# Gated DeltaNet decode step: two tokens per 32-row group, outer products on four row tiles, block inverse from NT directly

## The chip, the cores and the metric

The kernel runs on one core of a Trainium2 chip. Its metric is the device time of one launch in microseconds (us), the median of repeated runs.

## What is computed

One inference step of a two-layer hybrid decoder trunk in float32, for 256 new prompt tokens and 8 decode tokens (one new token for each of 8 sequences), so that every activation has 264 columns. Layer A is a gated DeltaNet mixer (32 value heads, 16 key heads, head size 128) and a SwiGLU block; layer B is sliding-window attention and another SwiGLU block. The change touches only the DeltaNet mixer. For the prompt it works in chunks, and needs the inverse of a unit triangular matrix for each head and chunk:

```python
a_mat = jnp.where(strict, jnp.einsum('bhnid,bhnjd->bhnij', kb, k) * decay, 0.0)
t_mat = lax.linalg.triangular_solve(a_mat + eye, eye, left_side=True, lower=True)
u = t_mat @ (v * beta[..., None]);  w = t_mat @ (kb * jnp.exp(gc)[..., None])
```

For the 8 decode tokens it carries a 128x128 state S for each token and head:

```python
S = S * jnp.exp(g_t)[..., None, None]
kv_mem = jnp.einsum('bhde,bhd->bhe', S, k_t)
S = S + jnp.einsum('bhd,bhe->bhde', k_t, (v_t - kv_mem) * b_t[..., None])
o = jnp.einsum('bhde,bhd->bhe', S, q_t)
```

## The kernel before

**Weights.** All weights pass through SBUF in 858 pieces of 128x1024 floats. ScalarE rounds a piece to `w_hi` (`split_hi`, line 470), VectorE computes the rest `w_lo` (`split_lo`, line 477), and TensorE multiplies each of the eight 128x128 tiles of a piece three times with 264 columns: `w_hi` by the high and the low part of the activations (lines 498 and 499, in turn), then, for all eight, `w_lo` by the high part (line 503). `w_hi` and `w_lo` have two buffers each, so `split_hi` of piece j+1 waits until TensorE is through with piece j-1.

**Turns.** The mixer runs in 16 groups G of two heads. In one turn of 12 pieces j = 0 to 11 TensorE projects the inputs of group g = G+1 while all engines do the DeltaNet work of group G in steps n = 0 to 23, two to a piece. On TensorE step 2j stands ahead of piece j and step 2j+1 in its middle, after 12 of its products. The last turn (G = 15) has no next group, and its pieces belong to the output projection. All engines take their instructions in the written order. ScalarE does at piece j: steps 4 or 16 where j is 2 or 8, then `split_hi` of piece j+1, then (j = 4, 8) the copies of the projection just ended (`unit_copy`), then steps 2j and 2j+1. VectorE does step 2j, then `split_lo` of piece j+1, then step 2j+1, with the convolution of group g (`conv`) and the decay and norm work (`early`) between; at j = 11 `split_lo` stands first.

**The inverse** (steps 2 to 14) starts from `NT`, the strictly upper matrices of four head and chunk pairs, each 128x128. Blocks of 16 are inverted by series (steps 4 to 7), and then blocks of 32, 64 and 128 are put together from two halves and the block of N between them (steps 8 to 14). Before the change `NT` is transposed on TensorE in step 7 (line 1975) into `Nm`, which ScalarE copies out (line 1709). `UF` is the finished inverse and lies in the same memory as `NT`. ScalarE writes its two 64x64 diagonal blocks for each matrix (line 1715), after which VectorE writes a 32x32 piece beside each (line 2372), and step 13 on TensorE (line 2008) waits for both through `inv_act` and `inv_dve`.

**The decode tokens** (steps 15 to 23): `kv_pad` holds k and v of the eight tokens, repeated three times at 32-column distance, and step 15 transposes it (line 2028). Step 17 multiplies the states by k and q of the tokens, eight products on four 32-column tiles (line 2051). VectorE copies the rows out to `kq_rows` (line 2419), and a product by the constant `gather` in step 18 (line 2062) puts them in place. `dec_d` is the error of the delta rule (lines 2397, 2399), `dec_sel` (line 2401) selects key and query rows, and the product of both (line 2076, step 19) is the output of the decode tokens. `kmask`, which GpSimd writes (line 1459), holds the keys of one token in each 128-column slice, as high part and rest in 96 rows, `dec_dr` holds the errors in like rows, and `outer` (line 1922) multiplies them, two tokens a call with 96 rows of contraction: calls 0 and 1 in step 21, call 2 in step 22, call 3 in step 23. VectorE adds the results to the states (`s_dec`, line 2437). `early` (lines 2107 and 2108), ahead of piece 11, sums the squares of the next keys in bank B[0]; step 23 sums the squares of the outputs (line 2096) and waits, among others, for ScalarE's logarithm of the former (`rn_ln`, line 1675).

## Time and profile before

| | |
|---|---|
| median of 3 runs | 2878.22 us (2877.65 to 2879.23) |
| span of the profiled execution | 2873.6 us |
| TensorE products busy | 2854.6 us, 99% |
| VectorE busy | 1795.8 us, 62% |
| ScalarE busy | 1417.1 us, 49% |
| GpSimd busy | 150.7 us, 5% |
| HBM traffic | 183 GB/s over the span |
| the 16 turns of the mixer | from about 71 to 900 us of the span |

The profiled execution gives its span, from its first to its last instruction, and no time of its own; the 4.6 us between the span and the median of the runs lie outside the instructions. PE is TensorE's products, PEld its weight loads, DVE VectorE, ACT ScalarE, POOL GpSimd. Recorded durations of products overlap their neighbours, so the time that a product takes of the engine is read from the start of the one to the start of the next.

### The profile page before, as it was taken

The page shows a single profiled execution, that of the slowest core. Times are in us where ns is not written, and L with a number is a line of the kernel's source. Part 1 is how long each engine was busy: PE and PEld are TensorE (multiplying, and loading weights), DVE is VectorE, ACT ScalarE, POOL GpSimd, SP SyncE. Part 2 cuts the span into 40 slices and gives each one's busy share as a digit, 9 for nine tenths or more (in the row PEclk, how much of TensorE's full clock was granted, in tenths as well). Part 3 has the DMA queues.
Part 4 walks back from the last instruction along what each step waited for, and adds up shares of the span by engine and source line. Part 5 has one row for each costly group of instructions (what it writes and reads, how often), then busy time and mean ns, then how long its engine had stood idle before and what let it go on. Part 6 is the DMA issues. An engine that isn't in the chain of part 4 may idle for free.

```text
span 2873.6 us, 68820 instructions
## 1 busy us (share of the span) xinstructions
PE 2854.6 (99%) x25511; PEld 2781.0 (97%) x25511; DVE 1795.8 (62%) x2900; ACT 1417.1 (49%) x2141; POOL 150.7 (5%) x285
## 2 busy tenths in 40 slices
PE   8999999999999999999999999999999999999999
PEld 7999999999999999999999999999999999999999
DVE  7888788888886455555555444587555555554444
ACT  6666566565664444444444343566444444444343
POOL 1112112111110000000000000000000000000000
PEclk9999999999999999999999999999999999999999
DMA  7666656666556555555555555744555555555554
GB/s 226 189 178 188 191 166 194 181 177 188 160 182 198 187 188 178 181 180 178 182 179 180 183 180 181 221 151 130 171 182 179 179 182 178 180 182 179 182 180 152
DMA packets 521091, 518.97 MB, mean 181 GB/s; under 512 B 32128, under 2 KB 444201, under 8 KB 520665
## 3 DMA queue, kind: packets, MB, share of 16 engines
q1 hardware_dynamic: 519150, 510.34, 57.6%
q0 software_dynamic: 1152, 5.58, 0.6%
q8 instruction: 147, 2.41, 0.4%
q10 hardware_dynamic: 594, 0.25, 0.0%
q14 instruction: 48, 0.39, 0.0%
HBM read 492.12 MB, written 32.82 MB: 183 GB/s over the span
## 4 chain that ended last, share of the span: by engine, by line
PE 67%; issue 1%; ACT 0%; DMA 0%; DVE 0%; DVEq 0%; ACTq 0%; POOLq 0%
PE bank L498 11%; PE bank L503 11%; PE bank L499 11%; PE upper L503 11%; PE upper L498 11%; PE upper L499 11%; PE upper L1027 0%; PE upper L1052 0%; DMA x_res<-x_spill 0%; PE upper L1038 0%; PE upper L1089 0%; PE upper L1028 0%; PE upper L1055 0%; ACT scores L812 0%; PE upper L1042 0%
## 5 line engine op out<-in xcount | busy, mean ns | idle before, releaser
L477 DVE TENSOR_TENSOR w_lo<-w_raw,w_hi 128x1024 fp32r<-128x1024 f32 x858 | 1051.2, 1225 | 919.9 <-ACT w_hi L470 917.0
L470 ACT ACTIVATE w_hi<-w_raw 128x1024 fp32r<-128x1024 f32 x858 | 910.1, 1061 | 1241.6 <-PE bank L503 709.1
L498 PE MATMUL bank<-h_hi,w_hi 128*128 128x264 f32 x3168 | 829.6, 295 | 0.4 <-DVE h_lo L585 0.3
L499 PE MATMUL bank<-h_lo,w_hi 128*128 128x264 f32 x3168 | 794.8, 284 | 0.0
L498 PEld LDWEIGHTS bank<-h_hi,w_hi 128*128 128x128 f32 x3168 | 597.3, 189 | 21.3 <-issue 8.8
L499 PEld LDWEIGHTS bank<-h_lo,w_hi 128*128 128x128 f32 x3168 | 598.2, 189 | 1.3
L503 PE MATMUL bank<-h_hi,w_lo 128*128 128x264 f32 x3168 | 449.8, 284 | 0.0
L503 PEld LDWEIGHTS bank<-h_hi,w_lo 128*128 128x128 f32 x3168 | 412.1, 188 | 0.0
L498 PE MATMUL upper<-h_hi,w_hi 128*128 128x264 f32 x1456 | 361.7, 285 | 0.0
L499 PE MATMUL upper<-h_lo,w_hi 128*128 128x264 f32 x1456 | 361.4, 284 | 0.0
L498 PEld LDWEIGHTS upper<-h_hi,w_hi 128*128 128x128 f32 x1456 | 274.3, 188 | 0.0
L499 PEld LDWEIGHTS upper<-h_lo,w_hi 128*128 128x128 f32 x1456 | 273.9, 188 | 0.0
L503 PE MATMUL upper<-h_hi,w_lo 128*128 128x264 f32 x1456 | 206.6, 284 | 0.0
L503 PEld LDWEIGHTS upper<-h_hi,w_lo 128*128 128x128 f32 x1456 | 189.3, 188 | 0.0
L498 PE MATMUL upper<-a_hi,w_hi 128*128 128x264 f32 x688 | 170.9, 284 | 0.0
L498 PE MATMUL bank<-a_hi,w_hi 128*128 128x264 f32 x688 | 170.9, 284 | 0.0
L499 PE MATMUL bank<-a_lo,w_hi 128*128 128x264 f32 x688 | 170.7, 284 | 0.0
L499 PE MATMUL upper<-a_lo,w_hi 128*128 128x264 f32 x688 | 170.7, 284 | 0.0
L498 PEld LDWEIGHTS upper<-a_hi,w_hi 128*128 128x128 f32 x688 | 129.7, 189 | 0.0
L498 PEld LDWEIGHTS bank<-a_hi,w_hi 128*128 128x128 f32 x688 | 129.7, 189 | 0.0
L499 PEld LDWEIGHTS bank<-a_lo,w_hi 128*128 128x128 f32 x688 | 129.5, 188 | 0.0
L499 PEld LDWEIGHTS upper<-a_lo,w_hi 128*128 128x128 f32 x688 | 129.5, 188 | 0.0
(447 smaller groups left out, 3655.5 us busy)
## 6 DMA issues: line engine op xcount, KB each, us to landing
w_raw<-in_w_gate_up_dram SPq DMA_DIRECT2D x704, 256.0 KB, 2.9
w_raw<-in_w_in_a_dram SPq DMA_DIRECT2D x388, 256.0 KB, 3.2
w_raw<-in_w_down_dram SPq DMA_DIRECT2D x352, 256.0 KB, 2.9
w_raw<-in_w_out_a_dram SPq DMA_DIRECT2D x128, 256.0 KB, 3.1
s_dec<-in_state_delta_dram SPq DMA_DIRECT2D x32, 512.0 KB, 6.1
out_dram<-s_dec SPq DMA_DIRECT2D x32, 512.0 KB, 4.9
w_raw<-in_w_q_b_dram SPq DMA_DIRECT2D x64, 256.0 KB, 3.1
w_raw<-in_w_o_b_dram SPq DMA_DIRECT2D x64, 256.0 KB, 2.9
```

The lines of the kernel that those rows point to most:

```text
L470: nc.scalar.activation(w_hi[:, s % SPL, :], w_raw[:, s, :], ACT.Copy).then_inc(hi_ready, 1)
L477: ops.tensor_tensor(w_lo[:, s % SPL, :], w_raw[:, s, :], w_hi[:, s % SPL, :].bitcast(F32), ALU.subtract).then_inc(lo_ready, 1)
L498: nc.tensor.matmul(bank[bk][:, 0:T], high(t), xh, start=first, stop=False)
L499: nc.tensor.matmul(bank[bk][:, 0:T], high(t), xl, start=False, stop=False)
L503: m = nc.tensor.matmul(bank[bk][:, 0:T], low(t), xh, start=False, stop=last)
```

## The change

The inverse no longer uses the transpose of `NT`: the transposes of step 7, `Nm` and its copy go, and steps 8 to 14 multiply the other factor, transposed by VectorE (`Tm`), by `NT` itself. ScalarE copies one half of `Um` into `Us`, and its copy of the diagonal blocks into `UF` moves from step 11 to step 12, since step 11 on TensorE now reads the part of `NT` that it overwrites. The transposes of the 32x32 pieces move from step 13 of VectorE to step 12.

In the decode part, each 32-row group holds two tokens with four rows each (key three times, query once), so that the states' products come out in the rows in which they are used. `gather`, `kq_rows` and their product go, and `dec_sel` and `dec_d` move from step 18 to step 17 of VectorE, ahead of `vn`. `kmask` is written by ScalarE (step 17) and VectorE (step 18) in place of GpSimd. The eight outer products have 32 rows of contraction each, on four row tiles, each tile with a bank of its own, all in step 21; `early` waits for the first four updates of the states.

```diff
-            def decode_keys(G):
-                pool.wait_ge(dec_dve, 11 * G + 2)
-                pool.tensor_tensor(kmask[:, :, :], bc(dec_kd.bitcast(F32), 1, NB),
-                                   sel8[0:96, :].unsqueeze(2).broadcast_to([96, NB, P]),
-                                   ALU.mult).then_inc(kmask_ready, 1)
...
                 elif n == 7:
...
                     nc.scalar.activation(twos(Um), pair23, ACT.Copy).then_inc(inv_act, 1)
-                    act.wait_ge(inv_pe, 13 * G + 7)
-                    nc.scalar.activation(Nm[:, :, :], B[0][:, :], ACT.Copy).then_inc(inv_act, 1)
-                elif n == 11:
-
-                    act.wait_ge(inv_dve, 15 * G + 10)
+                    for b in range(2):
+                        at, to = slice(HP * b, HP * (b + 1)), slice(HP * (1 - b), HP * (2 - b))
+                        m = nc.scalar.activation(Us[to, :, :], pair23[at, 1, :].rearrange("p (m n) -> p m n", m=2), ACT.Copy)
+                    m.then_inc(inv_act, 1)
+                elif n == 12:
+
+                    act.wait_ge(inv_pe, 12 * G + 9)
                     for b in range(2):
                         at = slice(HP * b, HP * (b + 1))
                         m = nc.scalar.activation(UF[at, :, at], Um[at, :, :], ACT.Copy)
                     m.then_inc(inv_act, 1)
-                elif n == 12:
-                    act.wait_ge(inv_pe, 13 * G + 11)
-                    nc.scalar.activation(Tm[HP:P, 2:4, :], Tm[0:HP, 2:4, :], ACT.Copy).then_inc(inv_act, 1)
...
                 elif n == 13:
+                    act.wait_ge(inv_dve, 15 * G + 13)
+                    nc.scalar.activation(Um[0:HP, 0:2, :], UF[HP:P, 0:2, HP:P], ACT.Copy).then_inc(inv_act, 1)
                     after(act, on_added, G)
                     nc.scalar.activation(q_sq[:, :], qk[:, 0, :], ACT.Square, scale=float(P * EPS ** 0.5)).then_inc(q_sq_ready, 1)
...
+                elif n == 17:
+
+                    act.wait_ge(dec_dve, 9 * G + 1)
+                    for r in range(2):
+                        m = nc.scalar.activation(kmask[:, r, :], dec_k, ACT.Copy, scale=k_first[r])
+                    m.then_inc(dec_act, 1)
                 elif n == 19:
-                    act.wait_ge(dec_dve, 11 * G + 7)
-                    nc.scalar.activation(dec_dr[:, :, :], dec_d[0:96, :, :], ACT.Copy).then_inc(dec_act, 1)
+                    act.wait_ge(dec_dve, 9 * G + 7)
+                    nc.scalar.activation(dec_dr[:, :, :], dec_d, ACT.Copy, scale=d_first).then_inc(dec_act, 1)
...
-                    for m_ in range(4):
-                        m = nc.tensor.transpose(B[0][:, m_ * P:(m_ + 1) * P], NT[:, m_, :], ident)
-                    m.then_inc(inv_pe, 1)
                 elif n == 8:
 
+                    inv(inv_dve, 8)
                     inv(inv_act, 6)
-                    each4(pair23, full(Nm), half(Um)).then_inc(inv_pe, 1)
+                    each4(pair23, full(NT), half(Tm)).then_inc(inv_pe, 1)
                 elif n == 10:
                     inv(inv_dve, 9)
-                    each4(pair01, half(Tm), half(Xm)).then_inc(inv_pe, 1)
+                    each4(pair01, half(Xm), lambda m_, b: (Um[block(b), m_, :] if m_ < 2 else Us[block(b), m_ - 2, :])
+                          ).then_inc(inv_pe, 1)
...
                 elif n == 11:
 
-                    inv(inv_dve, 10)
+                    inv(inv_dve, 11)
                     for m_ in range(4):
                         for b in range(2):
                             lo, up = quarter(b, 1), quarter(b, 0)
-                            m = nc.tensor.matmul(B[0][up, m_ * QP:(m_ + 1) * QP], Nm[lo, m_, up],
-                                                 Um[lo, m_, QP:2 * QP], start=True, stop=True)
+                            m = nc.tensor.matmul(B[0][lo, m_ * QP:(m_ + 1) * QP], NT[up, m_, lo],
+                                                 Tm[up, m_, 0:QP], start=True, stop=True)
...
                 elif n == 13:
 
                     inv(inv_act, 7)
-                    inv(inv_dve, 13)
+                    inv(inv_dve, 14)
                     for i in range(2):
                         for b in range(2):
                             m_ = 2 * b + i
-                            m = nc.tensor.matmul(B[3][block(b), i * HP:(i + 1) * HP], Nm[block(1), m_, block(0)],
-                                                 UF[block(1), m_, block(1)], start=True, stop=True)
+                            m = nc.tensor.matmul(B[3][block(b), i * HP:(i + 1) * HP], NT[block(0), m_, block(1)],
+                                                 Tm[block(0), m_, :], start=True, stop=True)
...
                     pe.wait_ge(dec_padded, 5 * G + 5)
-                    for i in range(3):
-                        nc.tensor.transpose(B[0][0:96, i * P:(i + 1) * P], kv_pad[:, i, :], ident)
-                    nc.tensor.matmul(B[0][0:96, 3 * P:3 * P + NB], kv_pad[:, 0, :], qk[:, 0, NP:T], start=True,
+                    for i, m_ in enumerate((1, 2, 0)):
+                        nc.tensor.transpose(B[0][:, i * P:(i + 1) * P], kv_pad[:, m_, :], ident)
+                    nc.tensor.matmul(B[0][:, 3 * P:3 * P + NB], kv_pad[:, 0, :], qk[:, 0, NP:T], start=True,
                                      stop=True).then_inc(dec_pe, 1)
                 elif n == 16:
...
-                    pe.wait_ge(dec_dve, 11 * G + 5)
-                    nc.tensor.matmul(B[1][:, 0:2 * P], gather, kq_rows[:, :, :], start=True, stop=True).then_inc(dec_pe, 1)
...
                 elif n == 21:
-                    pe.wait_ge(kmask_ready, G + 1)
-                    pe.wait_ge(dec_dve, 11 * G + 11)
+                    pe.wait_ge(dec_dve, 9 * G + 9)
                     pe.wait_ge(seq_act, 2 * G + 2)
-                    outer(0).then_inc(outer_pe, 1)
+                    pe.wait_ge(dec_act, 3 * G + 3)
                     pe.wait_ge(seq_dve, 7 * G + 7)
-                    outer(1).then_inc(outer_pe, 1)
-                elif n == 22:
-                    pe.wait_ge(outer_dve, 16 * G + 4)
-                    outer(2).then_inc(outer_pe, 1)
+                    for r in range(2):
+                        for c in range(4):
+                            at = slice(32 * c, 32 * c + 32)
+                            m = nc.tensor.matmul(B[c][:, r * 2 * P:(r + 1) * 2 * P], kmask[at, r, :], dec_dr[at, :, :],
+                                                 start=True, stop=True, tile_position=(32 * c, 0))
+                            if r:
+                                m.then_inc(outer_pe, 1)
                 elif n == 23:
                     pe.wait_ge(outer_dve, 16 * G + 8)
-                    outer(3).then_inc(outer_pe, 1)
                     pe.wait_ge(on_sq, G + 1)
                     pe.wait_ge(rn_ln, min(G + 1, GROUPS - 1) + 1)
...
                 if G is not None:
-                    pe.wait_ge(dec_act, 2 * G + 2)
-                    pe.wait_ge(seq_dve, 7 * G + 5)
+                    pe.wait_ge(outer_dve, 16 * G + 4)
                 nc.tensor.matmul(B[0][:, 0:T], ones_r[:, :], k_hl[:, 0, :], start=True, stop=False)
...
                     elif n == 7:
                         dve.wait_ge(inv_act, 9 * G + 5)
-                        nc.vector.transpose(Tm[:, 0:2, :], Um[:, 0:2, :])
-                        for b in range(2):
-                            at, to = slice(HP * b, HP * (b + 1)), slice(HP * (1 - b), HP * (2 - b))
-                            m = nc.vector.transpose(Tm[to, 2:4, :], Um[at, 2:4, :])
-                        m.then_inc(inv_dve, 1)
+                        turned(Tm, Um)
                     elif n == 8:
...
                     elif n == 11:
+                        got(9)
+                        nc.vector.tensor_copy(Xm[:, :, 0:QP], m4(B[0][:, 0:P])).then_inc(inv_dve, 1)
+                    elif n == 12:
                         got(10)
-                        nc.vector.tensor_copy(Xm[0:96, :, 0:QP], m4(B[0][0:96, 0:P])).then_inc(inv_dve, 1)
-                    elif n == 12:
-                        got(11)
                         dve.wait_ge(inv_act, 9 * G + 7)
                         for b in range(2):
                             at = HP * b
                             m = ts(UF[at:at + QP, :, at + QP:at + HP], m4(B[1][at:at + QP, 0:P]), -1.0, None, ALU.mult)
                         m.then_inc(inv_dve, 1)
+                        own(13)
+                        nc.vector.transpose(Tm[QP:HP, :, 0:QP], UF[0:QP, :, QP:HP]).then_inc(inv_dve, 1)
                     elif n == 13:
-                        own(13)
-                        dve.wait_ge(inv_act, 9 * G + 8)
-                        for b in range(2):
-                            at = HP * b + QP
-                            m = nc.vector.transpose(Tm[at:at + QP, 2 * b:2 * b + 2, 0:QP],
-                                                    UF[0:QP, 2 * b:2 * b + 2, QP:HP])
-                        m.then_inc(inv_dve, 1)
-                        got(12)
+                        got(11)
                         nc.vector.tensor_copy(Xm[:, 0:2, :], B[3][:, 0:P].rearrange("p (m n) -> p m n", m=2)
                                               ).then_inc(inv_dve, 1)
...
                     if n == 18:
-                        dve.wait_ge(dec_pe, 4 * G + 3)
-                        dve.wait_ge(dec_dve, 11 * G + 4)
-                        for h in range(2):
-                            stt(dec_d[0:96, h, :], B[1][0:96, h * P:(h + 1) * P], sc_eb[0:96, h, 2:3], dec_d[0:96, h, :],
-                                ALU.mult, ALU.add).then_inc(dec_dve, 1)
-                        nc.vector.tensor_copy(dec_d[96:P, :, :], h2(B[1][96:P, 0:2 * P])).then_inc(dec_dve, 1)
-                        for h in range(2):
-                            stt(dec_sel[:, h, :], ident[:, 96:96 + NB], sc_eb[:, h, 0:1], dec_qk[:, :], ALU.mult,
-                                ALU.add).then_inc(dec_dve, 1)
+                        dve.wait_ge(dec_act, 3 * G + 1)
+                        for r in range(2):
+                            m = stt(kmask[:, r, :], dec_k, k_rest[r], kmask[:, r, :].bitcast(F32),
+                                    ALU.mult, ALU.add)
+                        m.then_inc(dec_dve, 1)
                 elif n == 16:
 
-                    dve.wait_ge(dec_pe, 4 * G + 1)
-                    nc.vector.tensor_copy(dec_kd, B[0][0:96, 0:P]).then_inc(dec_dve, 1)
-                    dve.wait_ge(dec_dve, 11 * G + 1)
-                    tt(dec_kd[64:96], B[0][64:96, 0:P], dec_kd[64:96].bitcast(F32), ALU.subtract).then_inc(dec_dve, 1)
-                    tt(dec_d[0:96, :, :], h2(B[0][0:96, P:3 * P]), sc_eb[0:96, :, 1].unsqueeze(2).broadcast_to([96, 2, P]),
+                    dve.wait_ge(dec_pe, 3 * G + 1)
+                    nc.vector.tensor_copy(dec_k, B[0][:, 2 * P:3 * P]).then_inc(dec_dve, 1)
+                    tt(dec_d, h2(B[0][:, 0:2 * P]), sc_eb[:, :, 1].unsqueeze(2).broadcast_to([P, 2, P]),
                        ALU.mult).then_inc(dec_dve, 1)
-                    tt(dec_qk[0:96, :], B[0][0:96, 3 * P:3 * P + NB], ident[0:96, 0:NB], ALU.mult).then_inc(dec_dve, 1)
+                    tt(dec_qk[:, :], B[0][:, 3 * P:3 * P + NB], key_sel, ALU.mult).then_inc(dec_dve, 1)
                 elif n == 17:
                     dve.wait_ge(seq_pe, 7 * G + 4)
                     for h in range(2):
                         stt(rhs[:, h, :], B[0][:, h * P:(h + 1) * P], sc_n[:, h:h + 1], vtok[:, h, 1, :],
                             ALU.mult, ALU.add).then_inc(seq_dve, 1)
 
-                    dve.wait_ge(dec_pe, 4 * G + 2)
-                    nc.vector.tensor_copy(kq_rows[:, :, :], h2(B[1][:, 0:2 * P])).then_inc(dec_dve, 1)
+                    dve.wait_ge(dec_dve, 9 * G + 3)
+                    for h in range(2):
+                        stt(dec_sel[:, h, :], query_sel, sc_eb[:, h, 0:1], dec_qk[:, :], ALU.mult, ALU.add
+                            ).then_inc(dec_dve, 1)
+                    dve.wait_ge(dec_pe, 3 * G + 2)
+                    for h in range(2):
+                        stt(dec_d[:, h, :], B[1][:, h * P:(h + 1) * P], sc_eb[:, h, 2:3], dec_d[:, h, :],
+                            ALU.mult, ALU.add).then_inc(dec_dve, 1)
                 elif n == 19:
-                    dve.wait_ge(dec_act, 2 * G + 1)
-                    mid = dec_dr[32:64]
-                    tt(mid, dec_d[32:64, :, :], mid.bitcast(F32), ALU.subtract).then_inc(dec_dve, 1)
+                    dve.wait_ge(dec_act, 3 * G + 2)
+                    stt(dec_dr[:, :, :], dec_d, d_rest, dec_dr[:, :, :].bitcast(F32), ALU.mult, ALU.add
+                        ).then_inc(dec_dve, 1)
...
-                    for i in ((0, 1), (2,), (3,))[n - 21]:
-                        dve.wait_ge(outer_pe, 4 * G + (i + 1))
-                        for bb in range(2):
+                    for c in ((0, 1), (2,), (3,))[n - 21]:
+                        dve.wait_ge(outer_pe, 4 * G + (c + 1))
+                        for r in range(2):
                             for h in range(2):
-                                s = s_dec[:, h, 2 * i + bb, :]
-                                at = (2 * bb + h) * P
-                                stt(s, s, sc_eg[:, h, 2 * i + bb:2 * i + bb + 1], B[2 + i % 2][:, at:at + P],
+                                b, at = 4 * r + c, (2 * r + h) * P
+                                stt(s_dec[:, h, b, :], s_dec[:, h, b, :], sc_eg[:, h, b:b + 1], B[c][:, at:at + P],
                                     ALU.mult, ALU.add).then_inc(outer_dve, 1)
```

## Rows read from the trace of the kernel before

**Rows 1.** the page: busy time and share of the span, instructions.

```profile
PE 2854.6 (99%) x25511; PEld 2781.0 (97%) x25511; DVE 1795.8 (62%) x2900; ACT 1417.1 (49%) x2141; POOL 150.7 (5%) x285
```

**Rows 2.** busy time by stretch: us, PE, PEld, DVE, ACT, POOL, clock, DMA, GB/s.

```profile
105.00:889.00 784.00, 783.14 (x8250) 730.01 (x8249) 645.10 (x1397) 480.56 (x896) 131.46 (x238) 1.00 0.63 180
```

**Rows 3.** instructions of line 1998: duration, first and last start.

```profile
L1998 PE MATMUL upper<-Xm,Tm x256: 191/191/212, 93.7 to 871.5; 32*32 32x32 f32 x128
```

**Rows 4.** TensorE in order of time, one turn: start, duration, line, operation.

```profile
497.79 0.46 PE L1907 MATMUL upper<-Um,Pb 64*64 64x64 f32 x16
...
498.18 0.66 PE L1975 MATMUL upper<-masks,NT 128*128 128x128 f32 x4
...
498.59 0.36 PE L498 MATMUL bank<-h_hi,w_hi 128*128 128x264 f32 x1
...
500.22 0.46 PE L1907 MATMUL upper<-Um,Nm 64*64 64x64 f32 x16
...
507.79 0.44 PE L1998 MATMUL upper<-Xm,Tm 32*32 32x32 f32 x16
...
509.82 0.45 PE L2008 MATMUL upper<-NT,Nm 64*64 64x64 f32 x8
```

**Rows 5.** ScalarE in order of time, same turn.

```profile
503.81 1.06 ACT L470 ACTIVATE w_hi<-w_raw 128x1024 fp32r<-128x1024 f32 x1 [0.81 <-PE bank L503]
...
504.78 0.83 ACT L1715 ACTIVATE NT<-Um 64x256 f32<-64x256 f32 x2
...
507.96 1.06 ACT L470 ACTIVATE w_hi<-w_raw 128x1024 fp32r<-128x1024 f32 x1 [2.35 <-PE bank L503]
```

**Rows 6.** VectorE in order of time, same turn, the inverse.

```profile
498.73 0.31 DVE L2351 STREAM_TRANSPOSE Tm<-Um 128x128 f32<-128x128 f32 x1 [0.81 <-ACT Um L1707]
...
508.37 0.58 DVE L2372 TENSOR_SCALAR NT<-upper 32x128 f32<-32x128 f32 x2 [0.62 <-PE upper L1998]
```

**Rows 7.** TensorE in order of time, steps 17 to 19.

```profile
519.11 1.07 PE L2051 MATMUL upper<-s_dec,kq_diag 128*32 128x256 f32 x16
...
521.67 0.66 PE L2058 MATMUL upper<-vn,NT 128*128 128x128 f32 x4
...
522.17 0.60 PE L2062 MATMUL upper<-kq_rows,masks 128*128 128x256 f32 x2
...
522.73 0.28 PE L499 MATMUL bank<-h_lo,w_hi 128*128 128x264 f32 x1
...
524.06 0.38 PE L2068 MATMUL upper<-qdec,S 128*128 128x128 f32 x2
```

**Rows 8.** VectorE in order of time, steps 17 and 18.

```profile
521.48 0.42 DVE L2419 COPY kq_rows<-upper 128x256 f32<-128x256 f32 x1
...
521.81 0.87 DVE L2259 SCALAR_TENSOR_TENSOR cacc<-craw,convw,cacc 128x256 f32<-128x256 f32 x2
...
522.60 0.42 DVE L2390 TENSOR_TENSOR vn<-upper,sc_b 128x256 f32<-128x256 f32 x1
...
523.40 0.60 DVE L2397 SCALAR_TENSOR_TENSOR Pb<-upper,sc_eb,Pb 96x128 f32<-96x128 f32 x2
...
524.49 0.61 DVE L2401 SCALAR_TENSOR_TENSOR dec_sel<-masks,sc_eb,dec_qk 128x8 f32<-128x8 f32 x2
```

**Rows 9.** TensorE in order of time, steps 21 to 23.

```profile
528.74 0.64 PE L1922 MATMUL upper<-dec_dr,kmask 96*128 96x256 f32 x4
...
529.21 0.28 PE L498 MATMUL bank<-h_hi,w_hi 128*128 128x264 f32 x1
...
530.67 0.29 PE L2107 MATMUL upper<-k_hl,ones_r 128*128 128x264 f32 x1
...
532.99 1.06 PE L2096 MATMUL upper<-norm_sq,masks 128*128 128x264 f32 x4
```

**Rows 10.** VectorE and ScalarE in order of time, steps 20 to 22.

```profile
529.78 2.15 DVE L2437 SCALAR_TENSOR_TENSOR s_dec<-s_dec,sc_eg,upper 128x128 f32<-128x128 f32 x8
...
532.36 0.46 ACT L1675 ACTIVATE k_sq<-upper,bias_c 128x264 f32<-128x264 f32 x1
```

120 lines of the change are left out of this document (64 added, 56 removed).

## The prediction

> **What bounds the kernel now.** I read the page's first part, then the busy time by stretch, then one instruction's starts over all turns, and then one turn of each engine in order of time. TensorE is busy 2854.6 of 2873.6 us, and the other engines at most 62% [rows 1]. The stretch that holds the turns but the first and the last shows the same more sharply: TensorE is idle for less than 1 us of 784, at a granted clock of 1.00, and VectorE is busy 645 us, 82% [rows 2]. So in the turns the time is TensorE's queue of work, and an instruction taken from it is worth the step from its start to the next start, as long as nobody makes TensorE wait afterwards. The turns are alike: the block of line 1998, once a turn, starts first at 93.7 and last at 871.5, which is 15 periods of 51.8 us [rows 3]. I therefore work out one turn, in the times of the turn around 490 to 541 us, and multiply. Only the mixer's 16 turns are touched; the other two thirds of the span stay as they are. Start-up has smaller constants to load and one more small table instruction, neither of which I price: TensorE runs on weight pieces there.
>
> With VectorE at 82% and each step waiting for the one before, the second question is which of the many hand-overs has slack. This decides the case, since the change shortens TensorE's work by about 1.3 us a turn and also moves instructions on ScalarE and VectorE.
>
> **Part 1, the transposes of NT.** They take TensorE from 498.18 to 498.59, 0.41 us [rows 4]; they go. What is late next? Step 8 started at 500.22 and would start at 499.81. It needs VectorE's transpose of `Um`, which began at 498.73 and in its new, full width takes one instruction of some 0.45 us (the row has 0.31 for half the width), so it is ready at 499.2 [rows 4, 6]. ScalarE's two half copies into `Us` stand where one wide copy of `Nm` stood. Cover is 0.6 us; I take the whole 0.41 us as gained. The exits from tiled work into full products cost the same after the transposes as after the tiles, so the bounds are narrow: 0.35 to 0.45.
>
> **Part 2, the move of the copies into UF.** This is where I expect the loss. Before, ScalarE copied the diagonal blocks in step 11, at 504.78, in time in which it was idle anyway: its next instruction, `split_hi` of piece 7, started at 507.96, just behind the start of step 12 on TensorE at 507.79, for which it had waited 2.35 us [rows 4, 5]. In the new order the copies stand in step 12, and step 12 stands behind that `split_hi` in ScalarE's queue. They can't start before it is done. From the rows: `split_hi` at 507.96, the copies 0.97 us after it (504.78 less 503.81, the same pair of instructions), so at 508.93; they last 0.83, to 509.76 [rows 5]. VectorE's two scalings of the 32x32 pieces, which began at 508.37, now wait for them and last 0.58: 509.78 to 510.36. Behind them comes the transpose of these pieces, now in one instruction of 32x128, for which I take the 0.31 of the transpose with as many elements a row and 0.03 for the wait on its own predecessor: 510.70 [rows 6]. Step 13 on TensorE waits for it (the count of `inv_dve` is now 14). With 0.06 for the semaphore it starts at 510.76; it started at 509.82 [rows 4]. The loss is 0.94 us in each turn, at a place where TensorE has nothing else in its queue. Both step 12 and `split_hi` count from the same product's end, so that a turn that arrives earlier doesn't shorten it. Bounds: 0.83, if the copies and scalings overlap as neighbours sometimes do, and 1.1, if the restart of a stopped TensorE costs a weight load. Behind VectorE's wait stand `split_lo` of piece 7, half of the convolution and two of `early`; `split_lo` would end near 512, and the piece needs it after 515, so this is covered.
>
> **Part 3, the gather product and the new order on VectorE.** From the start of the product of line 2062 to that of the second weight product behind it are 0.56 us, and a weight product takes 0.12, so it costs 0.44; the block ahead of it, line 2058, took 0.50 to its next start where its like takes 0.45, since the product had waited for `kq_rows` [rows 7]. Together TensorE would be at step 19 by 0.49 us earlier: 523.57 in place of 524.06. But step 19 needs `vn`, and VectorE now does more ahead of it. Gone is the copy of `kq_rows`, 0.33 from start to start (521.48 to 521.81). In its place stand the two of `dec_sel`, 0.54, and the two of `dec_d`, 0.60, from step 18 [rows 8]. So `vn`, which began at 522.60 and took 0.42, is ready at 523.83 and TensorE goes on at 523.9. Of 0.49 us 0.16 is left. Bounds: 0 (were the small instructions slower for the 128 rows in place of 96) and 0.25 (were neighbours to overlap fully).
>
> **Part 4, the outer products.** Before: two calls in step 21, 0.47 us from 528.74 to 529.21, which is 0.12 for each product of 256 columns, and two more calls of some 0.24 to 0.3 in piece 11; about 1.0 us altogether [rows 9]. The price of eight products on row tiles of 32 isn't in the trace; the nearest is line 2051 with column tiles: eight products of plain float32 with 256 columns in 1.07 us [rows 7]. One such untiled product is 0.44 us (line 2062 above), so eight would be 3.5; the tiles work four at a time, and about 0.2 us is lost besides. For the new products, each 0.12 us, I take two rounds, 0.24, and 0.33 for this loss and the two changes of tiling: 0.57 us, 0.10 more than what stood in this place. From above the bound is eight in a row and the same loss, 1.3 us; from below 0.24.
>
> The Trainium skill, TensorEngine Tiling (Array Packing), Theoretical Speedup and Key Properties, gives up to four times the rate for a contraction of 32, and says that a change of tiling mode drains the engine. By the first alone the block would be 0.24 us; by the second too it comes near my 0.57, and the rows of line 2051 agree with both.
>
> But again this stretch isn't TensorE's. ScalarE goes without a gap from `split_hi` at the start of piece 10 through two table-bound functions to the logarithm at 532.36 to 532.82, and step 23 waits for it; it started at 532.99 [rows 9, 10]. VectorE updates the states from 529.78, eight in 2.15 us, so that the fourth ends near 530.9, and `early`, which came at 530.67, now has to wait for it, because bank B[0] takes one of the results. With the 0.16 us of part 3 all of this comes earlier by 0.16: fourth update 530.75 and `early` 530.83; two products 0.24 and twelve of 0.12 bring TensorE to step 23 at 532.5; the logarithm is there at 532.66 and step 23 starts at 532.72. This is 0.27 us earlier than before. So parts 3 and 4 together give 0.27 us a turn and not the 1.0 that TensorE is spared. Bounds: 0 to 0.45. Even products in a row (1.3 us) would only move this to 0.1. Behind this, VectorE is busy without a gap up to step 5 of the next turn and has about the same 0.1 to 0.2 us of slack there, so that no more than this can be passed on.
>
> **What costs nothing:** GpSimd's `kmask` (1.9 us) goes from an engine that idles. ScalarE's two `kmask` copies in step 17 stand before a wait of 1.5 us for piece 8. VectorE in steps 16 to 19 has some 0.3 us less. The state stores wait for all 16 updates as before.
>
> **The sum.** A turn: -0.41 + 0.94 - 0.27 = +0.26 us; fifteen turns +3.9. In the last turn there is no next group and so no convolution in VectorE's way; there I count the gather product in full and 0.4 us for the outer products: -0.41 + 0.94 - 0.49 - 0.4 = -0.36. Together +3.5 us: a span of 2877.1, and, with the 4.6 us outside it as before, 2881.7 us. By bounds a turn lies between -0.07 (0.83 less 0.45 less 0.45) and +0.75 (1.1 less 0.35), which is 2876 to 2889 us. About 0.2% (5.8 us) is what a measurement can tell from no change.
>
> **Rivals.** *The order of ScalarE's queue doesn't bite.* If step 13 isn't held, be it that `split_hi` of piece 7 can start earlier than I read it or that the scalings don't wait long, the turn gets -0.41 - 0.27, in all about -11.5 us: 2866.7. For it: the gain is plain work off a full engine. Against it: the 2.35 us wait in ScalarE's row. Half of the hold would give 2874. *VectorE's chain is the bound and pays nothing back.* If `dec_sel` and `dec_d` ahead of `vn` take 0.2 us more than the rows say, step 19 starts no earlier than before, and if each of the new waits (steps 13, 19, `early`, 23) costs a restart of about 0.1 us, a turn is +0.53 to +0.8, in all 2886 to 2890, slower than before. It decides from the point where `vn` is ready after 524.06 in the turn shown. *The tiles don't run side by side.* That would be 2884, inside my own case.
>
> **Chances.** My case 0.60 (2876 to 2884), the first rival 0.15 with its half form, the second 0.2, a loss elsewhere that I don't see 0.05. Faster by over 0.2% 0.14, within 0.2% 0.60, slower 0.26. Range 2872 to 2889, which leaves out the full form of the first rival and the end of the second.
>
> **What would show it.** In the new trace: no line with `Nm`; TensorE idle for about 0.9 us once a turn, ahead of the first product of step 13, released by VectorE's transpose; ScalarE's copies into `UF` right behind a `split_hi`; small waits of 0.2 to 0.3 us ahead of step 19 (for `vn`) and of `early` (for `s_dec`); the eight outer products within 0.6 us; a period of 52.0 us where it was 51.8. I am wrong if there is no idle time ahead of step 13, or if `vn` comes before TensorE does.

## Result and the profile after

The changed kernel takes 2886.14 us (2884.69 to 2887.95, nine runs); the kernel before takes 2877.65 us (2876.05 to 2879.51, nine runs beside them). The ratio is 1.003, with a 95% interval of 1.0021 to 1.004: the change makes the kernel slower by 8.5 us. It lies in the range of 2872 to 2889, but 2 us above the case that I held likeliest (2876 to 2884) and past the border of 0.2%, and so in the outcome to which I gave 0.26.

The page of the changed kernel, busy time, to be read beside [rows 1]:

```profile
span 2886.1 us, 68598 instructions
...
PE 2845.7 (99%) x25415; PEld 2763.0 (96%) x25415; DVE 1777.9 (62%) x2837; ACT 1425.7 (49%) x2189; POOL 136.2 (5%) x268
```

TensorE does 8.9 us less work and the span is longer. The busy time by stretch says where the rest went; it is the stretch of [rows 2] with the same columns:

```profile
105.00:889.00 784.00, 766.27 (x8106) 706.34 (x8105) 624.11 (x1325) 488.64 (x940) 118.65 (x223) 1.00 0.62 180
```

In the turns TensorE was idle for 0.9 us of 784 before and is idle for 17.7 us now, at the same granted clock of 1.00. The list of what TensorE waited for (us in total, times, the longest; three of its lines) names the place:

```profile
PE upper L2011 <- ACT Um L1725: 15.5, 16, 1.0
...
PE upper L510 <- DVE w_lo L484: 2.4, 1, 2.4
PE upper L2109 <- DVE s_dec L2432: 2.4, 14, 0.2
```

Line 2011 is step 13, sixteen times, once a turn. One turn of TensorE in order of time (start, duration, line, operation, idle time before); step 12 is line 2001, step 19 line 2070, the outer products line 2089, `early` lines 2109 and 2110, step 23 line 2099. A row that the view cut at the edge of its stretch counts only the instructions in it, as the last three `w_lo` products do here (535.28):

```profile
511.97 0.44 PE L2001 MATMUL upper<-Um,Xm 32*32 32x32 f32 x16
...
515.03 0.45 PE L2011 MATMUL upper<-Tm,NT 64*64 64x64 f32 x8 [0.96 <-ACT Um L1725]
...
528.82 0.41 PE L2070 MATMUL upper<-qdec,S 128*128 128x128 f32 x2
...
533.42 0.28 PE L506 MATMUL bank<-h_lo,w_hi 128*128 128x264 f32 x1
533.63 0.51 PE L2089 MATMUL upper<-dec_dr,kmask 32*128 32x256 f32 x8
534.07 0.39 PE L505 MATMUL bank<-h_hi,w_hi 128*128 128x264 f32 x1
534.29 0.29 PE L506 MATMUL bank<-h_lo,w_hi 128*128 128x264 f32 x1
...
535.28 0.52 PE L510 MATMUL bank<-h_hi,w_lo 128*128 128x264 f32 x3
535.97 0.36 PE L2109 MATMUL upper<-k_hl,ones_r 128*128 128x264 f32 x1 [0.17 <-DVE s_dec L2432]
536.17 0.28 PE L2110 MATMUL upper<-k_hl,ones_r 128*128 128x264 f32 x1
...
537.87 0.68 PE L2099 MATMUL upper<-norm_sq,masks 128*128 128x264 f32 x2
```

ScalarE and VectorE in the same turn, around the copies into `UF`, which answer to [rows 5] and [rows 6]:

```profile
512.14 1.06 ACT L477 ACTIVATE w_hi<-w_raw 128x1024 fp32r<-128x1024 f32 x1 [3.09 <-PE bank L510]
513.11 0.83 ACT L1721 ACTIVATE NT<-Um 64x256 f32<-64x256 f32 x2
514.58 0.31 ACT L1725 ACTIVATE Um<-NT 64x128 f32<-64x128 f32 x1 [0.65 <-DVE NT L2373]
...
513.97 0.58 DVE L2373 TENSOR_SCALAR NT<-upper 32x128 f32<-32x128 f32 x2 [2.03 <-ACT NT L1721]
514.58 0.30 DVE L2376 STREAM_TRANSPOSE Tm<-NT 32x128 f32<-32x128 f32 x1
```

This is the chain that was forecast, link by link. `split_hi` of piece 7 starts at 512.14, 0.17 us behind step 12; the copies follow at 513.11; VectorE's scalings, which waited 0.62 us for TensorE before, now wait 2.03 us for these copies; the transpose ends at 514.88 and step 13 starts at 515.03. From step 12 to step 13 it is 3.06 us where it was 2.03 [rows 4]. The wait is listed under ScalarE's line 1725, but in the kernel step 13 waits for VectorE's transpose of line 2376 and not for that copy; both start at 514.58 and end 0.01 us apart, and the list names the later one.

Where do 8.5 us come from? The 16 turns, from the first step 1 to the last step 12, take 806.1 us where they took 800.7: +5.4. The end of the span behind the last step 12 takes 2007.8 where it took 2002.1: +5.7. The start is 1.4 us longer, but it differs by up to 2.8 us between the profiled executions of these kernels. The two spans are 12.5 us apart, 4 us more than the medians: the profiled execution of the kernel before was shorter than the median of its kernel, and that of the changed kernel, with 2887.95 us, the longest of its nine. So the turns are shown at their full size (they differ by 0.2 us at most between two profiles of a kernel), and of the start and the end, 7.1 us in these two profiles, the medians hold only some 3.

### The profile page after: what moved, and what is told of

The parts are those of the page before. It is cut to its first block, busy times and chain, and to the rows that moved or that the text cites. A ratio compares the mean times of both kernels' runs of the same rounds, so it can differ in the third digit from the quotient of the medians.

```text
span 2886.1 us, 68598 instructions
## 1 busy us (share of the span) xinstructions
PE 2845.7 (99%) x25415; PEld 2763.0 (96%) x25415; DVE 1777.9 (62%) x2837; ACT 1425.7 (49%) x2189; POOL 136.2 (5%) x268
## 4 chain that ended last, share of the span: by engine, by line
PE 67%; ACT 1%; DMA 0%; DVE 0%; issue 0%; SPq 0%; DVEq 0%; ACTq 0%; POOLq 0%
PE bank L505 11%; PE bank L510 11%; PE bank L506 11%; PE upper L505 11%; PE upper L510 10%; PE upper L506 10%; PE upper L1034 0%; DMA x_res<-x_spill 0%; PE upper L1059 0%; PE upper L1045 0%; DMA out_dram<-S 0%; PE upper L1096 0%; DVE s_dec L2432 0%; PE upper L1172 0%; PE upper L1035 0%
```

## Experiments

Each is compared with the kernel before, run on the same chip in the same batch (its median lies between 2876.9 and 2877.7 us in the four batches); ratios have a 95% interval. "Turns" is the time from the start of the first step 1 to the start of the last product of the last step 12 in the profiled execution, "end" the span behind it. The last five kernels are made from "copies first".

| kernel | us | ratio | turns | end |
|---|---|---|---|---|
| before | 2877.65 | 1 | 800.7, 800.9 | 2002.1, 2002.7 |
| after | 2886.14 | 1.003 [1.0021, 1.004] | 806.1, 806.2 | 2007.8, 2007.3 |
| inverse only | 2888.17 | 1.0039 [1.0025, 1.0052] | 810.6 | 2004.3 |
| decode only | 2872.78 | 0.9987 [0.9978, 0.9996] | 796.8 | 2002.6 |
| before, copies late | 2888.91 | 1.0042 [1.0028, 1.0055] | 812.0 | 2003.3 |
| after, copies first | 2869.6 | 0.9973 [0.9963, 0.9984] | 790.8 | 2006.4 |
| + tiles in pairs | 2868.95 | 0.9969 [0.9957, 0.9982] | 790.4 | 2006.1 |
| + outer twice | 2869.42 | 0.9972 [0.9962, 0.9983] | 790.4 | 2004.8 |
| + `early` later | 2868.18 | 0.9968 [0.9956, 0.998] | 789.1 | 2005.4 |
| + `qdec` later | 2869.17 | 0.9973 [0.9963, 0.9984] | 790.8 | 2006.4 |
| + both later | 2862.41 | 0.9948 [0.9934, 0.9961] | 783.9 | 2005.6 |

### The cause: which edit holds step 13

**Copies first.** The changed kernel, with ScalarE's step 12 called ahead of `split_hi` of piece 7, as its steps 4 and 16 are in their pieces.

```diff
-                    if j in (2, 8) and G is not None:
+                    if j in (2, 6, 8) and G is not None:
                         step(G, 2 * j)
...
-                        if G is not None and n not in (4, 16):
+                        if G is not None and n not in (4, 12, 16):
                             step(G, n)
```

> The changed kernel, but ScalarE does its copies into UF (step 12) ahead of the split_hi of the same piece, in time in which it idles, instead of behind it. Theory A (the place of these copies in ScalarE's queue is what makes the changed kernel slow): step 13 on TensorE follows step 12 by 2.03 us as in the kernel before and not by 3.06, a turn lasts 51.1 to 51.2 us where the changed kernel has 52.16, and the time is 2886.1 less 16 times 1.03, 2869.6 us; if VectorE's chain swallows a part, up to 2873. Theory B (the decode part with its new order on VectorE and its waits is what costs): the time stays over 2880 us. Theory C (the end of the mixer costs several us by itself, where in the changed kernel's trace TensorE waits 2.4 us once near 922 us): that wait is still there, and the time is some 4 us above what 15 turns explain.

Measured: 2869.6 us, 16.5 us less than the changed kernel, or 1.03 us for each of the 16 turns. The line of step 13 is gone from the list of waits. ScalarE and VectorE of this kernel, in order of time:

```profile
500.75 0.84 ACT L1721 ACTIVATE NT<-Um 64x256 f32<-64x256 f32 x2 [1.39 <-PE upper L1993]
502.44 1.06 ACT L477 ACTIVATE w_hi<-w_raw 128x1024 fp32r<-128x1024 f32 x1 [0.85 <-PE bank L510]
...
502.86 0.58 DVE L2373 TENSOR_SCALAR NT<-upper 32x128 f32<-32x128 f32 x2 [0.61 <-PE upper L2001]
```

The copies now run at 500.75, as soon as TensorE's step 11 (line 1993) is through, in time in which ScalarE is idle before and after; VectorE's scalings wait for TensorE again, by 0.61 us, as in [rows 6]. TensorE's step 12 and 13 start at 502.28 and 504.31, 2.03 us apart, as before. So the copies cost nothing in themselves: the 1.03 us a turn are due to their place behind `split_hi`. The wait of 2.4 us near the end of the mixer (line 510) is still there.

**Before, copies late.** The same from the other side: the kernel before with nothing but ScalarE's copies into `UF` moved from step 11 to step 12.

```diff
-                elif n == 11:
-
+                elif n == 12:
                     act.wait_ge(inv_dve, 15 * G + 10)
...
                     m.then_inc(inv_act, 1)
-                elif n == 12:
                     act.wait_ge(inv_pe, 13 * G + 11)
```

> The kernel before with one edit: ScalarE's copies into UF move from step 11 to step 12, behind split_hi of piece 7. Nothing else is changed, the transposes of NT stay. Theory A: the copies end 1.97 us after step 12's start on TensorE, VectorE's scalings 0.6 us later, and step 13 comes at 2.6 us and not 2.03: +0.6 us a turn, 2877.65 + 9.4 = 2887 us. If the order on ScalarE is harmless: 2877.6 us.

Measured: slower by 0.42%, 12.0 us; the turns take 11.1 to 11.3 us more, 0.75 a turn where 0.6 was expected. What TensorE waited for, in this kernel, where step 13 is line 2006:

```profile
PE upper L2006 <- DVE NT L2370: 10.1, 16, 0.7
```

The move alone makes the loss. It is smaller than in the changed kernel by VectorE's transpose, which here isn't among what step 13 waits for (0.30 us, and it starts 0.61 behind the scalings).

**Inverse only** and **decode only** take each half of the change by itself. The halves touch different steps, so that each edit is the diff of the change, cut to its part: "inverse only" has steps 7 to 14 as after, with steps 15 to 23 and `early` as before, and "decode only" the other way round.

> The kernel before with the inverse part of the change alone (no transposes of NT, copies into UF in step 12), the decode part as before. Theory A: each turn gains 0.41 us by the transposes and loses 1.03 at step 13, +0.62 us, so a period of 52.38 and 2877.65 + 9.9 = 2887.6 us, slower than the whole change. Theory B: no more than the kernel before, 2871 to 2878 us.

> The kernel before with the decode part of the change alone (rows of two tokens, no gather product, outer products on four row tiles), the inverse as before. Theory A: the turn of the changed kernel is 0.39 us longer than before, of which the inverse is 0.62, so this part gives 0.23 us a turn: a period of 51.53 and about 2874 us. Theory B: 2881 us or more. Theory C: faster in the turns, but with a wait of TensorE of 2 us or more at the end of the mixer, so that the time is at or above that of the kernel before.

Measured: the inverse alone is slower by 0.39% (11.3 us; turns +9.8), with the same 15.5 us of waits ahead of step 13 in 16 times; that is 0.37 us saved and 1.03 lost in each turn. The decode part alone is faster by 0.13% (turns -4.0, or 0.26 a turn; my parts 3 and 4 together were 0.27). The two medians add to 7.2 us against 8.5 for the whole, within their intervals.

### What the outer products cost, and what holds the end of a turn

These run on the kernel "copies first". **Tiles in pairs** gives TensorE both products of a row tile in a row, in place of four tiles in turn:

```diff
-                    for r in range(2):
-                        for c in range(4):
+                    for c in range(4):
+                        for r in range(2):
```

> The kernel of e1 with one edit: the eight outer products are issued tile by tile (row tile 0 twice, tile 1 twice, and so on) in place of tile 0, 1, 2, 3 and again. If a product overlaps only a neighbour in the queue that is on another tile, five of eight slots of 0.12 us are left in place of two, and the block grows from 0.44 us (start to next start) to about 0.8; if the order within the block doesn't matter, it stays at 0.44. In the time, the next step waits for VectorE anyway, so that of 0.36 us only some 0.1 shows: 2869.6 to 2872 us; a TensorE that is the bound here would give 2875 us.

**Outer twice** runs all eight products two times; the second pass writes the same results again:

```diff
-                    for r in range(2):
+                    for k in range(4):
+                        r = k % 2
                         for c in range(4):
...
-                            if r:
+                            if k == 3:
                                 m.then_inc(outer_pe, 1)
```

> The kernel of e1 with the eight outer products done twice in the same place (the second pass writes the same results). It adds two rounds on four tiles, 0.24 us of TensorE a turn. Theory D (behind the outer products TensorE waits for VectorE's first state updates and then for ScalarE's logarithm, so the products' own time hardly counts): early starts at the same time, the turn grows by 0.05 us at most and the time by under 1 us, 2869.6 to 2870.6. If TensorE's queue is the bound there: +0.24 us a turn, 2873.4 us.

Measured: with the tiles in pairs the block takes 0.45 us from its first start to the next product's, against 0.44 in turn, and the time is the same: the order in which the tiles are given doesn't matter here. With sixteen products TensorE shows:

```profile
524.44 0.75 PE L2090 MATMUL upper<-dec_dr,kmask 32*128 32x256 f32 x16
525.12 0.39 PE L505 MATMUL bank<-h_hi,w_hi 128*128 128x264 f32 x1
```

0.68 us where eight take 0.44: eight more cost 0.24, which is 0.03 each, four side by side. And the turns take 790.4 us against 790.8. The 0.24 us of real work in each turn cost nothing: between step 19 and step 23 TensorE isn't what sets the time, as I had argued from [rows 10], and a shorter outer block should bring nothing either, since in the turn shown VectorE is in `split_lo` until 534.71 and couldn't start its updates sooner. A shorter block was not run.

**`early` later** is aimed at the two waits that stand there: `early` goes behind the first two tiles of piece 11, and step 23 behind all of its `w_hi` products.

```diff
-                    if g is not None and j == 11:
-                        early(g, G)
...
-                    tiles(pe, c, tl, 0, cut)
+                    if g is not None and j == 11:
+                        cut = 8
+                        tiles(pe, c, tl, 0, 2)
+                        early(g, G)
+                        tiles(pe, c, tl[2:], 0, 6)
+                    else:
+                        tiles(pe, c, tl, 0, cut)
```

> The kernel of e1, but the two products of early stand behind the first two tiles of piece 11 in place of ahead of it, and step 23 behind all eight tiles in place of six: each 0.5 us later in TensorE's queue, nothing removed. Theory D: the waits at early (0.17 us by the profile, about 0.3 by the starts of the products around it) and at step 23 (about 0.1) go, the turn falls from 51.14 to about 50.9, held up by VectorE's chain at step 5 of the next turn; 2865 to 2867.5 us. If VectorE or ScalarE set the pace of the whole turn already: 2869.6 us. If the later logarithm makes the keys late for step 1: slower than 2869.6.

Measured: 2868.18 us, just above the range expected; the turns take 789.1 us, which is 0.11 us a turn of the 0.24 hoped for. The waits at `early` are gone, and a new one stands at step 5 of the next turn. Of this kernel the list of waits, TensorE, and VectorE in order of time:

```profile
PE upper L1918 <- issue: 4.4, 14, 0.4
...
539.47 0.46 PE L1918 MATMUL upper<-Pb,PbT 64*64 64x64 f32 x16 [0.33 <-issue]
...
537.48 0.68 DVE L2334 TENSOR_TENSOR intraT<-upper,ET 128x512 f32<-128x512 f32 x1
538.08 0.62 DVE L2337 TENSOR_TENSOR qdec<-qk,egR 128x256 f32<-128x256 f32 x1
538.63 0.43 DVE L2341 STREAM_TRANSPOSE PbT<-Pb 128x256 f32<-128x256 f32 x1
538.99 0.38 DVE L2342 TENSOR_TENSOR Xm<-Pb,masks 128x256 f32<-128x256 f32 x1
539.29 1.22 DVE L484 TENSOR_TENSOR w_lo<-w_raw,w_hi 128x1024 fp32r<-128x1024 f32 x1
```

The profile has no name for the wait, only "issue". VectorE's rows have: the product of `Xm` starts at 538.99, ends at 539.37, and TensorE's step 5 starts at 539.47. VectorE goes without a gap up to there, and `qdec`, which TensorE doesn't need before step 19 (line 2070), stands ahead of it. So **both later** also moves `qdec` behind step 5's work, and **`qdec` later** does this alone, without the move of `early`:

```diff
-                    dve.wait_ge(qn_ready, G + 1)
-                    dve.wait_ge(et_exp, 3 * G + 3)
-                    tt(qdec[:, :, :], bc(qk[:, 0, P:2 * P], 1, 2), egR[:, :, :], ALU.mult).then_inc(qdec_ready, 1)
...
                         plus(Fm, Pa)
+                        dve.wait_ge(qn_ready, G + 1)
+                        dve.wait_ge(et_exp, 3 * G + 3)
+                        tt(qdec[:, :, :], bc(qk[:, 0, P:2 * P], 1, 2), egR[:, :, :], ALU.mult).then_inc(qdec_ready, 1)
```

> The kernel of e7 with one more edit: VectorE makes qdec (0.6 us, not needed before step 19) behind its second sum of step 5, in time in which it waits for TensorE, in place of step 3. In e7 VectorE is busy without a gap for 20 us up to step 5, where TensorE waits for it, 0.33 us a turn by the profile. Theory E (from the outer products to step 5 of the next turn VectorE's chain is the bound, and behind e7's edits it alone): that wait goes, with its restart some 0.4 us a turn, 2868.2 - 6 = 2862 us. If something else holds step 5 as well: no faster than 2867.

> The kernel of e1 with the edit to qdec alone, early and step 23 where they were. Theory E: in e1 TensorE comes to step 5 just when VectorE is ready, since it has been held before at early and step 23, so that a VectorE that is ready sooner changes nothing: 2869.6 us, a turn as in e1, the waits at early still there. If qdec's 0.6 us is what holds each turn: 0.4 us a turn less, 2863 us.

Measured: both together 2862.41 us, 0.52% faster than before and 23.7 us under the changed kernel; `qdec` alone 2869.17, where "copies first" has 2869.6. Starting from 790.8 us the turns go to 789.1 by the one edit, to 790.8 by the other, and to 783.9 by both: 1.7, 0 and 6.9. In the best version the stretch from 105 to 889 us has this row:

```profile
105.00:889.00 784.00, 782.36 (x8289) 725.33 (x8288) 639.43 (x1364) 502.26 (x959) 123.70 (x223) 1.00 0.63 183
```

TensorE is idle for 1.6 us of 784, where the changed kernel was idle for 17.7.

### Both kernels once more

To see what of the difference at the start and the end belongs to the kernels and what to an execution, each was run and profiled once more.

> The kernel before once more, for its profile. It tells whether the wait of some 2.4 us at the end of the mixer (the reload of x_res lands 9.3 us after its issue in the changed kernel and in e1, 6.8 to 7.0 us in the others) belongs to a kernel or comes and goes: if it comes and goes, this profile may show either, with the span 4 us longer where it is there; if it belongs to the changed kernel, this one lands in under 7.1 us again with a span of 2873 to 2876 us.

> The changed kernel once more, for its profile: the turns as before (52.16 us). In five profiles of kernels with the whole change the reload of x_res landed 7.6 to 9.3 us after its issue, in the four others about 7. If that is the kernel's, this one has over 7.5 us again and a stretch from the last step 12 to the end of 2005 us or more; if it comes and goes, it may be near 2003 us.

Measured: before again takes 2876.04 us, with a span of 2874.2 us, turns of 800.9 and an end of 2002.7; after again 2887.07, with 2885.3, 806.2 and 2007.3. So the longer end came again with the changed kernel, 4.6 to 5.7 us in two profiles of each. In the last turn the way from step 12 to step 23 takes 0.40 us more, step 13's hold included. The rest stands at one place behind the turns. TensorE of the changed kernel there, in order of time:

```profile
922.63 0.28 PE L506 MATMUL upper<-o_lo,w_hi 128*128 128x264 f32 x1
925.32 1.37 PE L510 MATMUL upper<-o_hi,w_lo 128*128 128x264 f32 x8 [2.41 <-DVE w_lo L484]
926.90 0.59 PE L505 MATMUL upper<-o_hi,w_hi 128*128 128x264 f32 x1 [0.20 <-ACT w_hi L477]
927.29 0.42 PE L506 MATMUL upper<-o_lo,w_hi 128*128 128x264 f32 x1
927.51 0.42 PE L505 MATMUL upper<-o_hi,w_hi 128*128 128x264 f32 x1
```

VectorE before it, first of the kernel before and then of the changed one, and the changed kernel's busy time in two stretches (clock is the third number from the end):

```profile
912.70 1.45 DVE L2507 TENSOR_TENSOR x_res<-x_res,bank 128x264 f32<-128x264 f32 x4 [2.47 <-DMA x_res<-x_spill]
```

```profile
922.68 1.45 DVE L2502 TENSOR_TENSOR x_res<-x_res,bank 128x264 f32<-128x264 f32 x4 [4.97 <-DMA x_res<-x_spill]
...
926.50:929.50 3.00, 2.79 (x13) 2.60 (x13) 2.62 (x5) 2.27 (x3) 0.00 (x0) 0.50 0.54 191
920.00:926.00 6.00, 3.59 (x30) 3.38 (x29) 2.58 (x5) 1.84 (x5) 0.00 (x0) 1.00 0.34 131
```

VectorE's in-order queue stands for 4.97 us, before 2.47, at an addition that needs a reloaded activation, and `split_lo` is queued behind it; the additional 2.5 us are TensorE's wait of 2.41 (in "after again" 4.40, and a wait of 1.93). Then comes a second price: after this pause the granted clock is 0.50, the lower of its two levels (1.2 in place of 2.4 GHz), and the products follow each other by 0.22 us (927.29, 927.51) and not 0.12. By starts: 2.57 us more than usual from 922.63 to 925.32; 0.60 in the eight `w_lo` products and the wait for `w_hi` behind them; and the next sixteen products take 3.29 us, from 926.90 to 930.19, where sixteen take 1.95 elsewhere: 1.34. That is 4.5 us, of which the kernel before has some 0.35 too, a wait for `w_hi`. With the 0.40 it is 4.5 of the 5.7 us by which the end of this profile is longer.

The fall of the clock doesn't come with every such wait: the profiles of after, after again, "copies first", "tiles in pairs" and "`qdec` later" have waits of 1.8 to 2.4 us there and all show it (ends of 2006.1 to 2007.8), "`early` later" has 2.3 us and doesn't (2005.4), and none with a wait of 1.4 us or less does. Why the load is late isn't settled. From issue to landing on GpSimd's queue it takes 6.9 and 7.0 us in the kernel before, 7.4 in "before, copies late", 7.1 and 7.2 in the halves "inverse only" and "decode only", 8.7 to 9.3 in six profiles of kernels with the whole change, but 7.6 and 8.3 in "outer twice" and "both later". The profiles have one difference beside the issue that nobody tested: VectorE's next `split_lo` starts 0.24 to 0.27 us after it in the four with the old decode part (6.9 to 7.4 us), and between 0.08 before and 0.07 after it in the nine with the new one (7.2 to 9.3). That no more than points at a neighbour, since 0.06 goes with 7.2 and 0.07 with 9.3. An earlier load was not tried either.

## Why the prediction was right or wrong, step by step

**Right: what bounds the kernel.** TensorE's queue does, and a loss of 1 us at a place where it stops is a loss of 1 us in the turn: the 16.5 us of step 13 (16 times 1.03) come back in full when the copies are put first.

**Right: the transposes.** From step 1 to step 12 the first turn takes 22.46 us in place of 22.87, and the others but the last 22.34 to 22.40 in place of 22.76: 0.39 less in the mean, where 0.41 was forecast, and the cover of 0.6 us holds.

**Right: the hold of step 13,** with its mechanism and 0.94 forecast against 1.03 measured. The 0.09 lie in the hand-over: from the end of the transpose, 514.88, to TensorE's start, 515.03, it is 0.15 us where I took 0.06, a figure that none of my rows had. The hold decides the sign: without it the change gains 0.27%, which is my first rival (2866.7 forecast, 2869.6 measured). That rival fits the kernel with the copies first, not the one that I had to forecast.

**Mis-sized: the small instructions ahead of `vn`.** VectorE in steps 17 and 18 of the changed kernel, beside [rows 8]:

```profile
526.68 0.36 DVE L2410 SCALAR_TENSOR_TENSOR dec_sel<-masks,sc_eb,dec_qk 128x8 f32<-128x8 f32 x2
526.96 0.61 DVE L2414 SCALAR_TENSOR_TENSOR Pb<-upper,sc_eb,Pb 128x128 f32<-128x128 f32 x2
...
528.26 0.42 DVE L2386 TENSOR_TENSOR vn<-upper,sc_b 128x256 f32<-128x256 f32 x1
```

The pair of `dec_sel` takes 0.28 us from start to start and not the 0.54 that I took, and `dec_d` 0.52 and not 0.60. So `vn` is ready at 528.68, and TensorE starts step 19 at 528.82, 0.11 us after the product before it, without a wait. I had named this as a sign of being wrong. From step 18 to 19 the turn saves 0.45 us where I counted 0.16.

My 0.54 was read rightly and was not the price of the pair. GpSimd of the kernel before in the same turn, and VectorE of it in the last turn, in which GpSimd does nothing beside:

```profile
523.90 1.04 POOL L1431 TENSOR_TENSOR NT<-masks,sc_b 128x512 f32<-128x512 f32 x1
```

```profile
887.78 0.36 DVE L2401 SCALAR_TENSOR_TENSOR dec_sel<-masks,sc_eb,dec_qk 128x8 f32<-128x8 f32 x2
888.06 1.22 DVE L477 TENSOR_TENSOR w_lo<-w_raw,w_hi 128x1024 fp32r<-128x1024 f32 x1
```

Where GpSimd's product of line 1431 ends 0.45 us after the pair's start, as here at 524.94, the pair takes 0.53 to 0.54 us; in the first turn, where it ends 0.36 us after it, 0.45; in the last turn, without it, 0.28, as everywhere in the kernels with the new decode part, in which GpSimd is idle at this point. The two halves show the same: 0.53 in "inverse only", 0.27 in "decode only". So the pair was held up by a neighbour on GpSimd, as far as the rows can say without a run that moves that product alone. Step 19 also speaks against the second rival: its condition, `vn` late, never held, though the time of 2886.1 lies in the band of 2886 to 2890 that I gave it; the time alone would have named the wrong cause.

**Right, but of no effect on the time: the outer products.** In their own place they cost 0.63 us, from the start of the weight product before, 533.42, to that of the weight product after, 534.29 less its own 0.12 and one other: 0.44 for the block and about 0.1 for each change of tiling, as 0.21 from 533.42 to 533.63 and 0.22 from 534.07 to 534.29 show beside the usual 0.12. I took 0.57. The rate of the Trainium skill, TensorEngine Tiling (Array Packing), Theoretical Speedup, shows in "outer twice": 0.03 us a product for four side by side; and the drains that its Key Properties name would lie in the 0.2 us that stay when this rate is taken out of 0.44, and in the two changes; no run takes them apart. For the time all this is idle: between step 19 and step 23 the logarithm and the state updates decide, as doubling the block showed.

**Missed in size: the waits at `early` and at step 23.** I had `early` wait until 0.08 us after the fourth update, and it is 0.2: eight updates take 2.14 us from 534.71, the fourth ends near 535.78, and `early` starts at 535.97. The profile's 0.17 us is not what this costs. By starts, the last `w_lo` product is at 535.53 (three from 535.28, 0.12 apart) and would be followed at 535.65; `early` starts at 535.97, and its second product 0.20 later in place of 0.12: 0.4 us. Step 23 started 0.17 us after the logarithm's end before, and I counted on 0.06; it now starts 0.26 after, at 537.87. Neither 0.08 nor 0.06 was in my rows. ScalarE's logarithm and VectorE's updates in this turn:

```profile
537.15 0.46 ACT L1679 ACTIVATE k_sq<-upper,bias_c 128x264 f32<-128x264 f32 x1
...
534.71 2.14 DVE L2432 SCALAR_TENSOR_TENSOR s_dec<-s_dec,sc_eg,upper 128x128 f32<-128x128 f32 x8
```

So from step 19 to step 23 the turn takes 9.05 us where it took 8.93, and behind it 0.08 more up to the next step 1. I had let this stretch become shorter by 0.11.

The Trainium skill, Perfetto Trace Analysis, Tensor Engine Instruction, says that TensorE's end time is estimated from the instruction's size. The trace fits: a product of 0.28 us is followed by the next 0.12 us after its start, and an idle time counted from such an end leaves out the first part of a wait.

**The two errors cancelled, and that was luck.** Parts 3 and 4 were forecast at -0.27 us a turn, and "decode only" has -0.26: 0.29 more was gained at step 19 and given back at `early` and step 23 (0.22) and ahead of the next step 1 (0.08). "Both later" frees what is held there: its turn takes 50.64 us where that of "copies first" takes 51.14. I had said that VectorE has 0.1 to 0.2 us of slack up to step 5 of the next turn and can pass on no more. That was right, and it was the limit: the turn gained more than 0.11 us only when `early` and `qdec` were both moved.

**What the sum missed.** Two things. The turns were forecast at +3.5 us from the first step 1 to the last step 12 (fifteen times 0.26, less the last turn's transposes) and take +5.4, since a turn is +0.39 and not +0.26: 0.09 of the difference is the hold, 0.02 the transposes, 0.01 parts 3 and 4, and the rest hundredths elsewhere. And the end was forecast at about 0 (0.94 - 0.49 - 0.4) and has 4.6 to 5.7 us in the profiles: a reload that comes late, VectorE's queue behind it, TensorE's wait and the lower clock that follows. I had looked at no row behind 900 us, because the change touches nothing there; VectorE's 2.47 us at the reload would have shown that nothing covers a later landing. What made it land later I couldn't have said then and can't now.

Last, I added 4.6 us outside the span, by setting one execution's span against the median of others; that these lie outside the instructions was wrong. Every run since shows 1.8 us between an execution's own time and its span, so that the one profiled stood some 2.2 us below the median of its kernel. I forecast a difference of 3.5 us and 8.5 came. Set against the execution's own time, the forecast would have been 2.8 us lower, so that this error made up for a part of what the sum missed: luck again.

## What to carry to other kernels

When an instruction is moved by one step in a program with in-order queues, look first at what now stands ahead of it on its own engine: here a 0.83 us copy that was free in step 11 cost 1.03 us in step 12, in each turn, because a `split_hi` of 1 us, which can start no sooner than TensorE comes to step 12 itself, stood ahead of it; calling it ahead of that instruction turned 0.3% slower into 0.27% faster. Where several waits stand one behind the other, each edit alone can show nothing or a little (1.7 and 0 us) and the two together 6.9: a kernel whose TensorE is 99% busy should be tested with the edits combined before one is dropped. A price read from one turn can hold a neighbour's work: the pair of `dec_sel` cost 0.54 us beside a GpSimd instruction and 0.28 without it, and the last turn of the same trace had shown that. And the stretch behind the change is to be read too: a load that lands some 2 us later costs its wait, and in five of six profiles a stretch at the lower clock as well.

## What the runs showed of the hardware that I had not expected

Two small VectorE instructions of 128x8 take 0.28 us together, though the one by itself is listed with some 0.2, and 0.54 us where a GpSimd product runs beside them. Eight products of 32 rows and 256 columns on four row tiles take 0.44 us and sixteen 0.68, whatever the order of the tiles. A reload through GpSimd's queue differed between 6.9 and 9.3 us from issue to landing in kernels that issue it at the same place. A single pause of 1.8 to 2.4 us of TensorE was in five of six profiles followed by a fall of the granted clock, in the changed kernel some 3 us at 0.50, in which sixteen products took 1.3 us more than elsewhere.
